# Eight query weight chunks into row slots, splits handed to VectorE, and four loads put behind the last row

## The reference, cut to what matters

```python
def peer(xn, w_pq, subkeys, peer_u, peer_v):
    q = (xt @ w_pq).reshape(T, PEER_HEADS, 2, PEER_QDIM // 2)
    s = jnp.einsum('thpd,hpnd->thpn', q, subkeys)
    top_s, top_i = lax.top_k(s, PEER_TOPK)
    ...
    best_s, best_pos = lax.top_k(cand_s.reshape(T, PEER_HEADS, kk), PEER_TOPK)
    expert = jnp.take_along_axis(cand_i..., best_pos, axis=-1)
    gate = jax.nn.softmax(best_s, axis=-1)
    act = jax.nn.gelu(jnp.einsum('thkd,td->thk', peer_u[eb], xb)) * gb
    out = jnp.einsum('thk,thkd->td', act, peer_v[eb])
```

## Time and profile before

| | |
|---|---|
| runs | 2516.51, 2516.71, 2528.49 us; median 2516.71 us |
| span of the profiled execution | 2449.2 us |
| expert stage, from the subkeys' load to the last `x_residual` add | about 416.6 to 1140 us |
| PE, DVE, ACT, POOL busy over the span | 2190.0, 1628.7, 997.5, 541.4 us |
| TensorE's mean granted clock over the span | 0.968 of full speed |

### The profile page before, as it was taken

How to read it: one execution, slowest core, us unless ns; L and a number is a source line. 1 busy time by engine, 2 the same in 40 slices (tenths; PEclk the granted TensorE clock), 3 DMA queues, 4 the chain that set the end, 5 groups by cost and what they waited for, 6 DMA issues and landing times. The chain is left out here.

```text
span 2449.2 us, 40856 instructions
## 1 busy us (share of the span) xinstructions
PE 2190.0 (89%) x16086; PEld 1805.2 (74%) x16086; DVE 1628.7 (66%) x3155; ACT 997.5 (41%) x1896; POOL 541.4 (22%) x549
## 2 busy tenths in 40 slices
PE   8988998877877777777999999999999898999998
PEld 7987998733332333224999988999999777888998
DVE  6675755766666676644766766666766777648666
ACT  5553535523333333333444445434444563024343
POOL 0000001877777777772100000000000000000000
PEclk9999999998899999999999999999999999999999
DMA  5530453899999999994655432655455432003653
GB/s 202 181 118 2 146 186 107 268 410 409 409 409 409 409 409 404 410 409 165 188 183 185 154 104 69 191 183 185 142 185 184 129 105 77 3 3 102 190 183 111
DMA packets 140319, 509.45 MB, mean 208 GB/s; under 512 B 15969, under 2 KB 16609, under 8 KB 139745
## 3 DMA queue, kind: packets, MB, share of 16 engines
q1 hardware_dynamic: 65824, 237.32, 30.4%
q0 software_dynamic: 73728, 268.47, 27.6%
q10 hardware_dynamic: 576, 1.05, 0.2%
HBM read 505.72 MB, written 1.05 MB: 207 GB/s over the span
## 5 line engine op out<-in xcount | busy, mean ns | idle before, releaser
L197 ACT ACTIVATE weights_high<-weights 128x1024 fp32r<-128x1024 f32 x436 | 460.2, 1059 | 532.5 <-PE ps L233 401.0
L231 PE MATMUL ps<-moving_high,weights_high 128*128 128x256 f32 x2224 | 639.8, 288 | 6.1 <-DVE moving_low L1277 3.0
L2284 PE MATMUL ps<-v_rows,subkeys 128*128 128x512 f32 x1024 | 494.7, 636 | 167.9 <-ACT subkeys L2338 167.9
L233 PE MATMUL ps<-moving_high,weights_low 128*128 128x256 f32 x2224 | 630.3, 283 | 0.0
L232 PE MATMUL ps<-moving_low,weights_high 128*128 128x256 f32 x2224 | 630.2, 283 | 0.0
L205 DVE TENSOR_TENSOR weights_low<-weights,weights_high 128x1024 fp32r<-128x1024 f32 x419 | 513.2, 1227 | 171.2 <-ACT weights_high L197 168.5
L2284 PEld LDWEIGHTS ps<-v_rows,subkeys 128*128 128x128 f32 x1024 | 200.6, 203 | 460.8 <-issue 460.7
L2444 DVE CUSTOM_DVE_ANT_0 u_rows<-u_rows,ps 128x1024 f32<-128x1024 f32 x256 | 308.9, 1219 | 233.2 <-DMA u_rows<-in_peer_u,experts 232.8
L231 PEld LDWEIGHTS ps<-moving_high,weights_high 128*128 128x128 f32 x2224 | 427.4, 192 | 11.4 <-issue 8.5
L232 PEld LDWEIGHTS ps<-moving_low,weights_high 128*128 128x128 f32 x2224 | 427.5, 192 | 0.6
L233 PEld LDWEIGHTS ps<-moving_high,weights_low 128*128 128x128 f32 x2224 | 427.1, 192 | 0.0
(11 more groups left out here) (569 smaller groups left out, 3198.2 us busy)
## 6 DMA issues: line engine op xcount, KB each, us to landing
weights<-in_l_ffn SPq DMA_DIRECT2D x264, 512.0 KB, 4.0
weights<-in_w_in SPq DMA_DIRECT2D x44, 512.0 KB, 4.0
weights<-in_l_in SPq DMA_DIRECT2D x24, 512.0 KB, 3.7
weights<-in_l_rkv SPq DMA_DIRECT2D x24, 512.0 KB, 3.6
weights<-in_w_ckv SPq DMA_DIRECT2D x16, 512.0 KB, 4.4
weights<-in_w_pq SPq DMA_DIRECT2D x16, 512.0 KB, 4.1
weights<-in_w_up_pair SPq DMA_DIRECT2D x8, 512.0 KB, 3.5
weights<-in_w_mix_out SPq DMA_DIRECT2D x8, 512.0 KB, 4.4
```

The source lines that it names most:

```text
L197: act.activation(self.high[:, c % SPLIT, :], self.raw[:, c % RING, :], ACT.Copy)\
L231: pe.matmul(out, lhs.high, rhs.high, start=start, stop=False)
L233: return pe.matmul(out, lhs.low, rhs.high, start=False, stop=stop)
L2284: last = pe.matmul(k.ps[:, 2 * tb + half, :], diagonal[:, i % DIAGONALS, :], v_rows[:, i % V_RING, 512 * half:512 * half + 512], start=i < ...
```

## The change

Four edits, all around the expert stage:
1. The last eight query chunks (8 to 15) aren't loaded through the raw ring. SP issues them at the stage's start, right behind the subkeys, into places 6 to 13 of `v_rows`, which hold no rows yet. ACT and the splitting engine read them there. The raw ring goes on with chunk 16 behind chunk 7, so chunks 16 to 19 wait for the splits of chunks 4 to 7.
2. POOL splits eight times in its loop (chunks 3 to 11) and issues pair 0 one split earlier. From pair 3 on nothing stands between its gathers; the `v` gathers of slots 6 to 13 wait for the split of the chunk that lay in their place.
3. DVE splits chunks 12 to 19: two ahead of `keys_of(1)` (with a wait until POOL has done chunk 11), two behind it, and one each ahead of slots 3, 5, 7 and 9.
4. SP waits for the last `v` row to land before it loads chunks 20 to 23.

```diff
+EARLY_CHUNKS = 8
...
+    def source(self, c):
+
+        return self.early_places[c - self.early] if self.is_early(c) else self.raw[:, c % RING, :]
...
+    def load_early(self, sp, places):
+
+        self.early_places = places
+        for c, place in enumerate(places):
+            sp.dma_start(place, self.plan[self.early + c]).then_inc(self.early_filled[c], 16)
...
         for c in range(self.loaded, min(first + count + SPLIT + RING, len(self.plan))):
-            if c >= RING:
-                sp.wait_ge(self.split, c - RING + 1)
+            if self.is_early(c):
+                continue
+            held = c - RING - (EARLY_CHUNKS if self.is_early(c - RING) else 0)
+            if held >= 0:
+                sp.wait_ge(self.split, held + 1)
...
-    FIRST_GATHER = 6
+    POOL_SPLITS, FIRST_GATHER, EARLY_SLOT = N // 2, 5, V_RING - EARLY_CHUNKS
...
             sp.dma_start(keys[:, :, :], k.dram["subkeys"]).then_inc(S["keys_loaded"], 16)
+            k.w.load_early(sp, [v_rows[:, EARLY_SLOT + c, :] for c in range(EARLY_CHUNKS)])
+            k.w.load_ahead(sp, first, N - RING)
+            last = SLOTS_ALL - 1
+            sp.wait_ge(k.v_ready[last % V_RING], 16 * (last // V_RING + 1))
             k.w.load_ahead(sp, first, N)
...
+                elif i >= EARLY_SLOT:
+                    pool.wait_ge(k.w.split, k.w.early + i - EARLY_SLOT + 1)
...
-            for n in range(N):
+            for n in range(POOL_SPLITS):
                 k.w.split_low(pool, first + n + 1)
-                if n >= FIRST_GATHER and n - FIRST_GATHER < U_RING:
+                if n >= FIRST_GATHER:
                     gather(n - FIRST_GATHER)
-            for i in range(min(N - FIRST_GATHER, U_RING), SLOTS_ALL):
+            for i in range(POOL_SPLITS - FIRST_GATHER, SLOTS_ALL):
                 gather(i)
...
+            v.wait_ge(k.w.split, first + POOL_SPLITS + SPLIT)
+            k.w.split_low(v, first + POOL_SPLITS + 2)
             keys_of(1)
+            k.w.split_low(v, first + POOL_SPLITS + 4)
             v.wait_ge(S["transposed"], 4)
             for i in range(SLOTS_ALL):
                 j, s = i // K, i % K
+                if i in (3, 5, 7, 9):
+                    k.w.split_low(v, first + POOL_SPLITS + 5 + (i - 3) // 2)
```

More of the change, by code:

```diff
@@ L204, in split_low @@
             v.wait_ge(self.rounded, c + 1)
-            v.tensor_tensor(self.low[:, c % SPLIT, :], self.raw[:, c % RING, :],
+            v.tensor_tensor(self.low[:, c % SPLIT, :], self.source(c),
                             self.high[:, c % SPLIT, :].bitcast(F32), ALU.subtract).then_inc(self.split, 1)
```

16 lines of the change are left out of this document (13 added, 3 removed).

## The result

The changed kernel takes 2512.98 us (median of 17 runs, 2508.09 to 2520.14), the kernel before beside it 2523.31 us (17 runs): a ratio of 0.997, 95% interval 0.996 to 0.9979, so a gain of 7.6 us by the ratio (5 to 10) and 10.3 by the medians. Forecast were 16.7 us and 2500.0. The sign was right, the size was not, and the time lies outside the range. Of the 13.0 us between 2500.0 and 2512.98, 6.6 lie in the kernel before (its median over 17 runs is 2523.31, over the three of the front table 2516.71) and 6.4 in the gain.

The account below looks back on a forecast made before the run. The expert stage was taken as bound by a full DMA (409 GB/s, 2.56 us a pair) behind a POOL-limited ramp; 17 us earlier less port trouble, taken as 16.7, cut 2516.7 to 2500.0 us, range 2495 to 2507.

Parts of the forecast that it names:

- The 67.5 us around it stay: Sum: the time between profiled span and median stays 67.5 us, so span 2432.5 becomes median 2500.0.
- Those last splits wait in turn for ACT: Ramp ahead of pair 6: POOL's last splits wait for ACT, which waits for chunks to land (2.57 us for chunk 19).
- Pair 0 at 441.7: Ramp start: pair 0 leaves at 441.7 instead of 444.5, with chunk 7 up to 2 us late for ACT.
- Pairs 1 to 5: POOL's ramp: pair 1 at 446.6 after 4.9 us, pairs 2 to 5 without a gap, the last by about 461.6.
- The 0.5 us of the sum: Port trouble between DVE's splits and POOL's gathers: bounded at 0 to 4.9 us, taken as 0.5 off the 17 us.
- Pair 6 at 463.6: Ramp: pair 6 leaves right behind dot 0 at about 463.6 instead of 480.42, 16.8 us earlier.
- Dots 5 and 9, margins of 0.7 and 0.9 us: DVE's ramp: dots 5 and 9 done at 475.1 and 485.2, with 0.7 and 0.9 us to spare for their pairs.
- the rival DVE or port: Ramp: tight dots slip 2 to 4 us or four gathers wait a split; gain 8 to 13 us, chance 0.13.
- Bytes alone: Ramp limited by the DMA's work, not POOL: only 12.8 us of weights leave, 2503.9 us; chance 0.05.
- More: Ramp weights cost their 6.00 MB at 300 GB/s, 20 us, since mixed queues run slower; 2496.7 us; chance 0.05.
- Undone: Last loads or waits undo the gain, early places freed late or pairs behind DVE; no change, 2516 us; chance 0.03.
- slower: Gathers hold DVE's eight splits 8.3 us each, 66 us less 16.7: 2566 us; chance 0.04.

Follow-up runs that it names:

- seven_first: Changed kernel with SP loading chunk 7 behind three of the eight early loads instead of all; 2517.46 us, ratio 0.9971 to the kernel before.
- undo_held: Changed kernel with chunks 20 to 23 loaded among the rows as in the kernel before; 2517.79 us, ratio 0.9974 to the kernel before.
- b_again: The kernel before, unchanged, profiled a second time; 2525.72 us (one run), span 2523.9.
- after_again: The changed kernel, unchanged, profiled a second time; 2433.56 us where the kernel before took 2450.28, ratio 0.9937.
- loads_only: Changed kernel's early and held loads alone, POOL splitting and issuing as in the kernel before; 2451.66 us, ratio 1.0001 to the kernel before.
- late_splits: Changed kernel with DVE's splits of chunks 16 to 19 moved to slots 18, 20, 22, 24; ratio 1.0011 to the kernel before, in the repeat (late_splits_b) 1.001.
- plain_rows: late_splits with slots 3 to 13 filled by SP's plain loads of consecutive rows instead of gathers (wrong output); 2426.98 and 2430.94 us.
- half_rows: late_splits with the gathers of slots 6 to 13 fetching half rows (wrong output); 2433.26 and 2433.37 us.
- gate4: late_splits with pair 4 and all behind it waiting for TensorE's last query chunk; ratios 0.9977 and 0.998 to the kernel before.
- paced: seven_first and late_splits together, pairs 3 to 7 each waiting for one more used chunk; ratios 0.9939, 0.995, 0.9956 and 0.9939 to the kernel before.

## Why the prediction was wrong

**Mechanism and size.** At 2450 both held: 15.4 to 16.7 us gained (12 to 19 by the interval) against 16.7 forecast, pair 16 at 74.4 behind S instead of 89.0, 14.6 us earlier. The forecast came from a profile at that level, and it is right for it. The step that failed is the transfer, "The 67.5 us around it stay". The true distance between an execution and its own span is 1.8 to 2.0 us (2525.72 and 2523.9; 2512.98 and 2511.0; 2433.87 and 2431.9). 67.5 us was therefore not what lies around the span but another kind of execution, and the profile could not tell what the change does to it. That distance was the warning in the front table: read rightly, it says that the runs to be forecast are not the ones profiled, and the range should have been wider. What the runs showed in its place: at 2525 pair 16 goes out 2.3 us earlier and not 16.5, because TensorE slows beside the gathers and dot 5 waits for it. That the sign still came out right isn't the mechanism's merit, since most of the gain at that level lies behind pair 16, where the prediction says that nothing differs.

**Two readings.** "Those last splits wait in turn for ACT" is wrong: the earlier trace rows has the four splits in 9.27 us without a pause, and chunk 19 was rounded by 476.42, ahead of its split. ScalarE's waits for weights didn't reach GpSimd there. The range's lower end, 2495, is called the larger gain's edge, but 19 us give 2497.7 and the 20 us of the rival 2496.7.

**Pair 0 at 441.7**, 25.1 behind S: 26.5 (26.4 at 2450). Chunk 7 came later than the 2 us allowed: ScalarE waited 3.84 us and rounded it at 436.03, not 433, and GpSimd stood 6.06 us. seven_first gets the 1.5 us back in the trace, and not in the time.

**Pairs 1 to 5**: 4.98 and 4.80 us for the first two steps, as costed (4.9), then 3.5, 2.5 and 2.5. Two gathers took 1.48 and 1.93 us beside VectorE's splits instead of 0.94. Each ends 0.8 to 0.9 us behind the first split beside it (the split from 454.37 to 455.59, the gather until 456.43; 462.39 to 463.6 and 464.42), so it is held until the split is over. The row at 495.07 that bounded this was the right one. The Trainium skill ("SBUF — State Buffer", Who interferes with whom) infers that such an operation leaves descriptor writes alone; these rows disagree, unless a gather counts as an instruction that reads SBUF (it takes its row numbers from `experts`), which by the same section does contend. No run tells the two apart. These two cost nothing, since pair 6 waits for dot 0 anyway, but at 2450 the gathers of 1.48, 1.12 and 1.88 us behind it do: pair 16 follows pair 6 by 26.5 us (468.22 to 494.74) and not by 24.9. With pair 6's 0.8 us (next) that is why it left at 74.4 behind S and not at 71.9 (488.5 less 416.56). The 0.5 us of the sum should have been 1.6.

**Pair 6 at 463.6**, 47.0 behind S: 47.9 (466.16 less 418.21) and 47.8. Right to 1 us at both levels, and released by dot 0 as said.

**Dots 5 and 9, margins of 0.7 and 0.9 us.** Right at 2450: there pair 12 waits 0.30 us for a dot and no other gap is over 0.5. At 2525 this is where it broke, and by another cause than the rival DVE or port named: that one priced the dots' slips at 2 to 4 us, from held splits or a late chunk. Dot 5 came 10.4 us late because TensorE did. The prediction costed TensorE only as a customer of splits ("PE needs chunk 12's low part at about 457") and never asked whether it could be slowed by what the rows do around it. That rival's gain, 8 to 13 us, is about what came (7.6 or 10.3), for a reason it did not have: that is luck.

**409 GB/s from 466.** At 2450 it is 391 from 466 to 468 us and 409 from 500 on. At 2525 it is 341 to 391 in the slices, and the row stream waits for TensorE and VectorE again and again: in b_again 74.9 us ahead of v gathers alone. "In that regime no engine's saving counts" doesn't hold at this level.

**Held loads at no cost.** Right: undo_held equals the changed kernel within the interval. SP issues them in 1.75 us at 1194.45 (at 1120.41 in after_again), and ScalarE rounds chunk 20 at 1221.95 and 1147.77 without a wait.

**The rivals.** Bytes alone (12.8 us) is refuted, for the level of the profile, by loads_only's 1.0001. More (20 us) is refuted for the same reason, since it rests on the weights as well. Undone and slower did not come; eight splits on VectorE were never held 8.3 us.

**The accounts at 2525.** From S to pair 16 the change wins 2.3 us there (89.0 to 86.7) instead of 14.6. The two single executions differ by 12.9 us in span: 1.1 by when the stage is reached, 2.3 to pair 16, and 9.3 behind it, where all the changed kernels of the table are 3 to 9 us shorter than b_again. Of those 9.3, GpSimd's waits for dots make up 8.8: 24.6 us in b_again behind slot 14, 15.8 in the changed kernel. But they are 21.9 in undo_held and 12.2 in late_splits_b, so they differ from execution to execution. Why the row part is shorter is not settled: most of the 10 us that the timed runs gain at this level lies there, and no run explains it.

**What slows TensorE** is not settled either. Shown is: in the query part it happens at 2525 alone; it begins when pairs leave each 2.5 us and the DMA passes 350 to 420 GB/s; it ends when they stop; and a longer run of them (late_splits) makes it longer. Not the clock, which falls after it. Nor is full pace always enough: among b_again's rows TensorE is busy 10.00 of 10 us from 505 to 515, beside 410 GB/s. The clock doesn't make the level either, as far as sums tell: it is 0.947 to 0.951 of full speed in the profiles at 2525 and 0.967 to 0.974 at 2450, but the changed kernel's row matmuls are busy only 18 us longer (509.0 against 491.1), while the rows behind pair 16 take 71 us longer (681.4 against 610.7). Instructions that arrive late would look like this, and TensorE's idle time is put down to "issue"; but a fetch stuck behind rows isn't seen. The queues of the changed kernel from 458 to 494 us (packets, MB, share):

```profile
q0 software_dynamic: 2851, 10.39, 77.6%
```

No packet of an instruction queue lies there, not even at 484 to 488, when the DMA moves nothing and TensorE is at work; one came at 455 to 458 and the next at 494 to 497. On the other level none lies between 460 and 482 either. So no packet was held up in the DMA; a fetch that waits before it becomes a packet would not be seen. Bytes, descriptors or the writes into SBUF remain. plain_rows, half_rows, gate4 and paced were made to tell these apart, and each met only the level at which there is nothing to tell.

## What to carry to other kernels

Before a profile is used to forecast a median, compare its span with the runs: here the distance is 2 us within an execution, and 67.5 us meant another level, with other waits. A transfer stream that is full is only bound by itself as long as the engines around it keep their pace: when its start is packed tighter, ask what else runs beside it at that moment and who feeds whom in a ring (here rows, TensorE, rounding, split, dot, rows). And try the parts alone before crediting them: the loads moved out of the way were worth nothing by themselves, and the splits that seemed to cause the stall were what limited it.

## What the hardware showed that I had not expected

- Two levels of the same program: spans of 2431.9 and 2511.0 us for one kernel. Runs made one after another nearly all shared a level (the exceptions are 2524.99 us among gate4's runs and 2535.43 among loads_only's), and the same chip was seen at both.
- At the slower one, in the query part, gathers at full pace leave TensorE 5.09 busy us of 20 beside 408 GB/s; beside the early weights, which a hardware queue brings, it is not slowed, as the changed kernel shows at 2525 (columns as in the stretches above):

```profile
420.00:430.00 10.00, 9.97 (x85) 9.77 (x85) 4.01 (x24) 6.06 (x11) 8.34 (x4) 1.00 0.99 405
```

  Nor is it beside gathers at a pair per 4.9 us (b_again).
- SP issues eight loads of 512 KB in 4.27 us, 0.53 each, where the earlier trace rows has 0.74.
- A gather beside VectorE's two-input splits takes up to 1.93 us instead of 0.94, and ends 0.8 to 0.9 us behind the split.
